# Sparse attention with a scan beside it: the second half of the scan's states moves from GpSimd to VectorE

## What is computed

```
# attention, for each block of 128 queries and each head
logits = einsum('bqhd,bqkd->bhqk', qb, kg) * a_scale     # masked to the chosen keys
p = softmax(logits);  o = einsum('bhqk,bqkd->bqhd', p, vg)

# scan: 32 groups of 16 channels, 64 complex states per group
b = coef * einsum('gnp,blgp->blgn', B, u)
s = associative_scan(_complex_combine, (abar, b), axis=1)          # s[t] = abar * s[t-1] + b[t]
y = einsum('gpn,blgn->blgp', C_re, s_r) - einsum('gpn,blgn->blgp', C_im, s_i) + D_skip * u
y = gelu(y);  y = y * sigmoid(y @ w_glu + b_glu)
```

## Time and profile before

| | |
|---|---|
| median of 3 runs | 3916.5 us (3909.71 to 3976.51) |
| the profiled execution | 3910.52 us, its span 3908.8 us |
| TensorE busy | 3665.5 us, 94% |
| VectorE busy | 2537.2 us, 65% |
| ScalarE busy | 1819.5 us, 47% |
| GpSimd busy | 1219.0 us, 31% |
| the stage of the change | from 437 to 697 us of the span |

### The profile page before, as it was taken

How to read it: one execution, slowest core, us unless ns; L and a number is a source line. 1 busy time by engine, 2 the same in 40 slices (tenths; PEclk the granted TensorE clock), 3 DMA queues, 4 the chain that set the end, 5 groups by cost and what they waited for, 6 DMA issues and landing times. The chain is left out here.

```text
span 3908.8 us, 53307 instructions
## 1 busy us (share of the span) xinstructions
PE 3665.5 (94%) x19688; PEld 3115.3 (80%) x19688; DVE 2537.2 (65%) x4296; ACT 1819.5 (47%) x3398; POOL 1219.0 (31%) x1199
## 2 busy tenths in 40 slices
PE   7999789898999999999999978899999999999898
PEld 6868666777888788788878877778899999999876
DVE  6679664346777576312675578876567777776666
ACT  3256466135333345321444457755445555545444
POOL 1423320141111101111235451100566666666400
PEclk9989999999999999999999989999999999999999
DMA  4322221562676574521235587855211111111064
GB/s 153 113 81 92 92 50 68 183 211 88 207 256 231 196 273 138 162 103 49 79 122 180 172 184 140 168 199 167 53 33 53 46 39 44 55 39 44 22 243 140
DMA packets 348750, 485.37 MB, mean 124 GB/s; under 512 B 45435, under 2 KB 219036, under 8 KB 344636
## 3 DMA queue, kind: packets, MB, share of 16 engines
q1 hardware_dynamic: 311580, 371.33, 30.2%
q0 software_dynamic: 34608, 106.45, 9.4%
q10 hardware_dynamic: 2304, 4.20, 0.3%
HBM read 337.43 MB, written 144.47 MB: 123 GB/s over the span
## 5 line engine op out<-in xcount | busy, mean ns | idle before, releaser
L119 PE MATMUL banks<-l_first_ws,l_XT 128*128 128x256 f32 x2880 | 359.6, 284 | 0.0
L119 PEld LDWEIGHTS banks<-l_first_ws,l_XT 128*128 128x128 f32 x2880 | 348.8, 192 | 0.0
L119 PE MATMUL banks<-l_XT,hg_ws 128*128 128x512 f32 x1440 | 343.2, 394 | 0.0
L119 PEld LDWEIGHTS banks<-l_XT,hg_ws 128*128 128x128 f32 x1440 | 266.7, 189 | 52.5
L4898 POOL TENSOR_TENSOR hg_DD<-hg_BB 128x256 f32<-128x256 f32 x224 | 173.9, 776 | 259.3 <-PE banks L4651 133.4
L4751 DVE TENSOR_TENSOR hg_DD<-hg_Q,hg_DD 128x256 f32<-128x256 f32 x224 | 204.7, 914 | 73.3 <-ACT hg_DD L4824 73.2
L119 PE MATMUL even_bank<-l_first_ws,l_XT 128*128 128x512 f32 x888 | 207.8, 392 | 3.2 <-PEq L909 1.9
L119 PE MATMUL even_bank<-even_ws,l_XT 128*128 128x512 f32 x876 | 204.4, 390 | 0.0
L119 PEld LDWEIGHTS even_bank<-l_first_ws,l_XT 128*128 128x128 f32 x888 | 167.3, 189 | 41.2 <-issue 6.0
L119 PEld LDWEIGHTS even_bank<-even_ws,l_XT 128*128 128x128 f32 x876 | 163.9, 188 | 34.0
L119 PE MATMUL am_g_acc<-l_XT,am_ws 128*128 128x512 f32 x768 | 176.1, 391 | 0.0
(11 more groups left out here) (771 smaller groups left out, 9213.8 us busy)
## 6 DMA issues: line engine op xcount, KB each, us to landing
l_first_raw<-in_odd_w_in SPq DMA_DIRECT2D x64, 512.0 KB, 5.5
l_first_raw<-in_even_w_in SPq DMA_DIRECT2D x16, 1024.0 KB, 5.4
l_room_tiles<-hidden SPq DMA_DIRECT2D x63, 256.0 KB, 6.9
da_first_X<-q_k_hi POOLq DMA_DIRECT2D x24, 512.0 KB, 8.0
da_first_X<-q_k_lo POOLq DMA_DIRECT2D x24, 512.0 KB, 13.1
l_room_tiles<-y_even SPq DMA_DIRECT2D x45, 256.0 KB, 5.7
ffn_y<-in_w_ffn_down SPq DMA_DIRECT2D x22, 512.0 KB, 4.5
weight_sums_w_ffn_down<-ffn_y SPq DMA_DIRECT2D x11, 1024.0 KB, 4.2
```

The lines of the kernel that those rows point to most:

```text
L119: mm = pe.matmul(out, lhs(p, k), rhs(q, k), start=start and i == 0, stop=stop and i == n - 1, skip_group_check=skip)
```

## The change

GpSimd's two generators are gone with their semaphores. `scan_states` on VectorE runs the same 17 steps for the first half and then for the second. In the loop VectorE takes two steps in each of the items 16 to 23 and one in every other item from 8. Sums 0 to 3 stand two items earlier on TensorE and VectorE (items 28 to 31 for 30 to 33), the clearing of `z` stands at item 23 for 25, and sums 4 to 7 stay at items 35 and 36. Counting the `next` calls, `scanned` rises to 1 in item 20 for 27 before, and to 2 in item 34 for 31 before.

```diff
@@ attend_and_scan: the tables @@
-        place[(30 + k, 1) if k < 4 else (35 + (k - 4) // 2, k % 2)] = SUM_OUT + k
+        place[(28 + k, 1) if k < 4 else (35 + (k - 4) // 2, k % 2)] = SUM_OUT + k
...
-    BACK_AT, ZERO_AT, BEFORE = 19, 25, S_C - 1
+    ZERO_AT, BEFORE = 23, S_C - 1
...
@@ GpSimd's program @@
-                def rotate_in():
-                    pool.wait_ge(in_moved, 8)
...
-                    link.mark(pool.tensor_tensor(p1t, wr, er, ALU.mult))
-                    yield
-                    link(pool.tensor_tensor(p2t, wi, ei, ALU.mult))
-                    yield
-                    link(pool.tensor_tensor(zr, p1t, p2t, ALU.add))
-                    yield
...
-                def rotate_back():
...
-                    pool.wait_ge(scans_run, 2)
-                    pool.wait_ge(x_split, 6)
-                    link.mark(pool.tensor_tensor(p1t[:, :, 0:BEFORE], zr_, er_, ALU.mult))
-                    yield
...
                 for n in range(ITEMS + 2):
-                    if n >= SCAN_AT:
-                        next(inward, None)
-                    if n >= BACK_AT:
-                        next(back, None)
                     if n == ZERO_AT:
                         pool.wait_ge(scanned, 1)
                         pool.memset(z[:, :, 0:HALF], 0.0).then_inc(zeroed, 1)
@@ VectorE's program, scan_states @@
+                    for e, (zr, zi) in enumerate((first_half, second_half)):
+                        j = slice(e * S_J // 2, (e + 1) * S_J // 2)
+                        wr, wi, er, ei = w[:, 0, j, :], w[:, 1, j, :], decay[:, 0, e], decay[:, 1, e]
+                        link.mark(dve.tensor_tensor(t1, wr, er, ALU.mult))
                         yield
+                        link(dve.tensor_tensor(t2, wi, ei, ALU.mult))
                         yield
+                        link(dve.tensor_tensor(zr, t1, t2, ALU.add))
                         yield
+                        link.mark(dve.tensor_tensor(t1, wi, er, ALU.mult))
                         yield
+                        link(dve.tensor_tensor(t2, wr, ei, ALU.mult))
                         yield
+                        link(dve.tensor_tensor(zi, t1, t2, ALU.subtract))
                         yield
+                        link(dve.tensor_copy(t1, m8[:, j].unsqueeze(2).to_broadcast([P, S_J // 2, S_C])))
+                        link(dve.memset(t1[:, :, 0:1], 0.0))
+                        yield
+                        for q in range(2):
+                            zf = z[:, q, e * HALF:(e + 1) * HALF]
+                            link(dve.tensor_tensor_scan(zf, F[:, 5, :], zf, 0.0, ALU.mult, ALU.add))
+                            yield
...
+                        link(dve.memset(w[:, :, j, 0:1], 0.0))
+                        link.mark(dve.tensor_tensor(x1, zr, er, ALU.mult))
+                        yield
+                        link(dve.tensor_tensor(x2, zi, ei, ALU.mult))
+                        yield
+                        for a in range(2):
+                            rows = slice(a * S_N, (a + 1) * S_N)
+                            link.mark(dve.tensor_tensor(w[0:S_N, a, j, 1:S_C], x1[rows], x2[rows], ALU.subtract))
+                            yield
...
+                        link.wait()
+                        dve.sem_inc(scanned, 1)
@@ VectorE's loop over the items @@
                     if n >= SCAN_AT:
-                        next(steps, None)
+                        for _ in range(2 if N <= n < N + 8 else 1):
+                            next(steps, None)
```

More of the change, by code:

```diff
@@ L2563, in store @@
                     pool.dma_start(yT[h * P:(h + 1) * P, half], yo[:, half]).then_inc(out_st[q], DMA)
-                inward, back = rotate_in(), rotate_back()
                 for n in range(ITEMS + 2):
-                    if n >= SCAN_AT:
-                        next(inward, None)
-                    if n >= BACK_AT:
-                        next(back, None)
                     if n == ZERO_AT:
@@ L2763, in scan_states @@
-                    x1, x2 = t1[:, :, 0:BEFORE], t2[:, :, 0:BEFORE]
-                    link(dve.memset(w[:, :, j, 0:1], 0.0))
-                    link.mark(dve.tensor_tensor(x1, zr, er, ALU.mult))
-                    yield
-                    link(dve.tensor_tensor(x2, zi, ei, ALU.mult))
-                    yield
-                    for a in range(2):
-                        rows = slice(a * S_N, (a + 1) * S_N)
-                        link.mark(dve.tensor_tensor(w[0:S_N, a, j, 1:S_C], x1[rows], x2[rows], ALU.subtract))
-                        yield
@@ L2773, in scan_states @@
-                    link.wait()
-                    link.mark(dve.tensor_tensor(x1, zr, ei, ALU.mult))
-                    yield
-                    link(dve.tensor_tensor(x2, zi, er, ALU.mult))
-                    yield
-                    for a in range(2):
-                        rows = slice(a * S_N, (a + 1) * S_N)
-                        link.mark(dve.tensor_tensor(w[S_N:P, a, j, 1:S_C], x1[rows], x2[rows], ALU.add))
-                        yield
-                    link.wait()
-                    dve.sem_inc(scanned, 1)
@@ new lines, in scan_states @@
+                        link.wait()
+                        link.mark(dve.tensor_tensor(x1, zr, ei, ALU.mult))
+                        yield
+                        link(dve.tensor_tensor(x2, zi, er, ALU.mult))
+                        yield
+                        for a in range(2):
+                            rows = slice(a * S_N, (a + 1) * S_N)
+                            link.mark(dve.tensor_tensor(w[S_N:P, a, j, 1:S_C], x1[rows], x2[rows], ALU.add))
+                            yield
```

70 lines of the change are left out of this document (3 added, 67 removed).

## The result

The changed kernel took 3917.9 us (median of 20 runs, 3907.9 to 3927.8) and the kernel before 3910.8 us (median of 20, 3905.6 to 3976.5; the one at 3976.5 stands apart, the other 19 end at 3916.5). The ratio is 1.0017 with a 95% interval of 1.0010 to 1.0023: slower by 4 to 9 us. The forecast was 3913 us and no change of any size.

What follows compares the result with a forecast made beforehand. VectorE was taken to bound items 8 to 23, TensorE the wide blocks after. -2.8 + 2.5 + 0 = -0.3 us took the profiled 3910.5 to 3910.2 us; 3913 us was given as the median, range 3899 to 3928.

Steps and rivals of the forecast that it cites:

- Everything behind sum 4 keeps its distances: Program after sum 4: later work follows it with unchanged spacing, so no change of pace to the end.
- Contention on VectorE: Items 8 to 23: removing GpSimd's products shortens VectorE's operations, by 10.1 us in the first stretch and 5.9 in the second.
- The late second half: Items 28 to 34: second half's weights issued at 554.9 us, landed 7.1 us later, so the 8.1 us lead is given back.
- gain at sum 4: Start of sum 4 on TensorE: 562.0 us instead of 564.82, a gain of 2.8 us.
- TensorE's wait: Ahead of sum 4: TensorE ready at 555.9 us, waits 6.1 us for the second half's weights.
- The clock after the wait: Sums 4 to 7 on TensorE: half clock behind the wait costs 2.5 us, between 0 and 5.5.
- third rival: The clock takes it all, chance 0.1: sums 4 to 7 wholly at half clock, 5.5 us, net +2.7 us.
- The stage's sum: Whole stage: -2.8 at sum 4, +2.5 for the clock, 0 for clearing `z`, together -0.3 us.
- three rivals: Lead kept, sum 4 8.9 us early (0.25); slower, +4.7 us (0.25); clock takes it all, +2.7 us (0.1).
- The second, *slower: Chance 0.25: the second half ends later than 557.7 us; 2 us delay plus full 5.5 us clock price, +4.7 us.
- The clearing of `z`: GpSimd's 1.80 us memset, moved into items 20 to 23: costs VectorE 0, or 1.1 us if it contends.

Runs made afterwards that it cites:

- e2: Changed kernel with the 4 MB residual load cut into eight loads: 3911.6 us, the 800 to 850 us piece 49.3 us.
- e7: Changed kernel with two scan steps in all items 16 to 31 and the residual load in eight pieces: 3908.5 us, ratio 0.9998 to the kernel before.
- e9: Changed kernel with the residual load in eight pieces and two scan steps in items 16 to 25 instead of 16 to 23: 3910.6 us.
- e10: Changed kernel with GpSimd clearing a spare 128x512 tile twice ahead of the residual load: the 800 to 850 us piece took 49.3 us.
- e11: Kernel before with the residual load issued ahead of GpSimd's first subtraction instead of behind it: ratio 1.0004, the 800 to 850 us piece 53.3 us.
- e6: Changed kernel with the four semaphores kept and 14 one-column clears on GpSimd: stage 159.3 us, the 800 to 850 us piece 52.9 us.
- e12: Kernel before with 24 one-column clears on GpSimd, each with a wait, at items 8 to 31: ratio 1.0006.
- e13: Changed kernel with 24 one-column clears on GpSimd, each with a wait, at items 8 to 31: residual load first, its first packet 2.1 us after issue.
- e14: Kernel before with 24 one-column clears on VectorE, each with a wait, in items 8 to 31: stage 2.7 us longer than before.
- e4: Changed kernel with two scan steps in each of items 16 to 31, not 16 to 23 alone: stage 153.8 us.
- e8: Changed kernel with sums 0 to 3 moved back to items 30 to 33: stage 160.4 us.
- e1: Changed kernel, unaltered, timed again on another chip: 4 us slower than the kernel before, ratio 1.0007 (0.9998 to 1.0016).
- e3: Kernel before with the residual load cut into eight loads: the 800 to 850 us piece took 49.4 us.
- e5: Kernel before, unaltered, timed again: ratio 0.9997, the 800 to 850 us piece 49.0 us.

## Why the prediction was wrong

The whole time is inside the range, but the forecast was no change, and the kernel is slower by 0.17%.

**The step that failed** is the last of the sum: "Everything behind sum 4 keeps its distances". From 850 us on, and between 627 and 800, it does. From 800 to 850 us it doesn't: 55.6 us for 49.8 in the profiles, and 52.2 to 55.7 in the six profiles with the change and a whole residual load, against 49.0 to 50.9 in four without the change. Against the 49.8 that is 2.4 to 5.9 us, the largest difference that every profile shows; how much is added to TensorE's waits by the half clock sets where in this range it lies. The cause of this piece's length is shown from both sides: take the early residual load away (e2, e7, e9, e10) and the changed kernel has 49.3 to 49.5 us; put it into the kernel before (e11) and that has 53.3. I had looked for what waits on the stage's engines, and not for two transfers that are issued together elsewhere and race for the DMA engines. The rows that could have warned me were in the trace: the residual's and the third chunk's issues 0.5 us apart, and ScalarE's wait of 4.57 us for that chunk. No wait of TensorE followed from it in the kernel before. Why the changed kernel's load comes first was not found. The distances of the issues are the same to 0.01 us, and at the lengths tried in e6, e12, e13 and e14 neither the number of GpSimd's instructions nor that of VectorE's turned the order.

**Contention on VectorE**: right. 10.1 us were forecast for items 8 to 15, and the stretch is 10.1 us shorter; the operations have the lengths forecast. Item 28 is transposed at 529.18, on the scale of before 531.7, for a forecast of 531.6.

**The late second half**: right in its mechanism, and a little dearer. The weights are issued at 552.9, or 555.4 on the scale of before, for 554.9. They land 8.3 us later and not 7.1, the figure that I took from the queues' falling idle in the kernel before. There too the last of them landed 8.4 us behind the first issue (554.91 to 563.28 us), so this was a misread row and not a slower load. So the gain at sum 4 is 1.0 us instead of 2.8: 0.5 from the issue and 1.2 from the landing. This term was mis-sized, and so is the forecast's sum. That the lead is bounded by this wait is shown by e4, where it is gone and the stage gains 3.4 us, and by e8, where it is longer and the stage loses 2.5.

**TensorE's wait** was 4.5 us and not 6.1, although the weights came 1.8 us later than forecast, because TensorE itself was 3.4 us later (556.7, or 559.3 on the scale of before, for 555.9). It had waited 1.90 us for a mask at 549.69, which the forecast does not have, and the values behind that took 5.30 us for the 3.62 us of e4. The granted clock had been down once before the wait (0.76 in 552.0 to 556.7 us), was 0.99 in it, and fell again as it ended.

**The clock after the wait**: 2.5 us were forecast, 0 to 5.5 the ends. The first sum ran at half the clock (pairs of matmuls of 0.63 us for 0.39) and from 565.29 on they are at full. The price in the profile is 18.6 - 16.9 = 1.7 us. It is not the same each time: with the same steps and sums it is 1.4 us in e1 and e13, 1.7 in e10, and 3.0 in e2 and e6, where the second sum is slow too (2.6 us for 1.95). The Trainium skill, page "TensorE: Matmul & The Clock Gate", section "HAM oscillation — how this bites in real kernels", has the wait send the array to half rate, and the trace agrees. But the array was back at full rate after one sum of four, or within the second, so the 5.5 us of the third rival was too dear.

**The stage's sum**: -0.3 us were forecast. The profiles give +0.6. Over all runs that leave the change's steps and sums where they are, the stage took 157.4 to 159.3 us (mean 158.2 of after, e1, e2, e6, e10 and e13) against 157.2 to 157.9 without the change (mean 157.6 of before, e3, e5, e11 and e12). The two above 159 are e2 and e6, by the clock price just named. So inside the stage "no change" was right within a microsecond or two, with the mis-sized landing and the smaller clock price partly making up for each other, and none of the three rivals came true as it was told. The second, *slower*, had the right sign and the wrong place. That the whole time still fell into the stated range says little, since the range is 29 us wide.

**The clearing of `z`** cost nothing that shows: it runs at 504.31 us for 1.81 us beside VectorE's operations, which all have their 1.21 to 1.23 us. The DVE rows above, and this one of GpSimd:

```profile
504.31 1.81 POOL L2522 MEMSET aa_three<- 128x2048 f32 x1 [0.49 <-DVEq L2727]
```

## What to carry to other kernels

A change in one stage can go with a loss far behind it, where nothing was edited: compare two traces piece by piece over the whole program, by the number of the matmul, before you look for the loss in the stage that was changed. Where a large load with no haste is released by the same event as a small one that is waited for, their order can turn with nothing in the times of issue to show it: issue the large one later or in pieces, and then time the change again, since otherwise you measure the tie. And a lead won by taking contention off VectorE lasts only if the moved work's own due time is met; here the second half's weights came 4.5 us after TensorE was ready for them, and half a remedy (e9) brought 0.5 us where the whole one (e4) brought 3.4.

## What the runs showed of the hardware that was not expected

Two transfers issued 0.5 us apart on two queues did not share the DMA engines evenly. In the 2 us window, the 512 KB of weights and the rows of its chunk had 90 to 95% of the engines' time against 4 to 6% where they began first (before, e5), and 31% against 57 to 68% where the residual did (e1, after). Part of this is that the second had not begun for some of the window. But where both had, it is no more even: in the 0.6 us behind the residual's first packet, 59 packets of the chunk went out and 6 of the residual (before, 802.88 to 803.5 us), and in the last 1 us of the other window 1 of the chunk and 84 of the residual (after, 800.92 to 801.92). The Trainium skill, page "DMA: Bandwidth & Descriptors", section "Queues, rings and completion order", says that each DMA engine takes turns between the queues that it has work for, a whole packet of several descriptors at a time. No even turns are to be seen in these stretches in either order. Whether the second queue had its packets ready is not shown, and no run here looked at a single engine.

The order did not look like chance: ten profiles of eight kernels fell into two groups without an exception, although the three issues keep their distances to 0.01 us. If the order is a property of the kernel, timing it more often does not average it out; whether it turns between executions of one kernel is not shown beyond the two profiles each of before and after.
